# A scan over chunks: spread rows for the decays, gates of the cells turned ahead, cell norm on ScalarE

## What is computed

```
z_a, xbc, dt_raw, z_b, q, k, v, ig, fg, og = split(rmsnorm(x) @ ab_w_in)
# state space mixer: xbc = silu(causal_conv(xbc)); xs, bm, cm = split(xbc); 16 heads of 64, 2 groups
y_a = y_diag(decays, cm, bm, xs * dt) + (cm @ state) * exp(acs) + xs * d_skip
state = state * exp(acs_end) + bm^T @ (decay_to_end * xs * dt)
y_a = rms(y_a * silu(z_a)) * ssd_norm_g                   # rms over each group of 512
# matrix memory mixer: q, k = silu(causal_conv(..)); 4 heads, keys of 128, values of 256
num = (q k^T * w_intra) @ v + w_inter * (q @ c_mem);  den = the same with ones for v
h = num / max(|den|, exp(-m_t)) * sigmoid(og)
c_mem = dec * c_mem + (g * k)^T @ v
y_b = rms(h) * ml_norm_g * silu(z_b)                      # rms over each head of 256
x = x + concat(y_a, y_b) @ ab_w_out
```

## Time and profile before

| | |
|---|---|
| median of 3 runs | 1576.92 us (1575.18 to 1577.39) |
| the profiled execution | 1573.38 us, span 1571.6 us |
| PE busy | 1525.6 us, 97% |
| DVE, ACT, POOL busy | 907.6, 649.0, 566.1 us |
| granted clock, mean | 0.992 |
| projection | 17 to 559 us |
| scan | 561 to 737 us |
| output product in the scan's stage | 737 to 761 us |

### The profile page before, as it was taken

One profiled execution on the slowest core, in us unless ns is written; L12 is line 12 of the kernel. 1 busy time (PEld: TensorE's weight loads), 2 busy tenths in 40 slices (PEclk: granted clock), 3 DMA queues, 4 the chain that ended last, 5 costly groups with the idle time before them and its releaser, 6 DMA issues.

```text
span 1571.6 us, 23657 instructions
## 1 busy us (share of the span) xinstructions
PE 1525.6 (97%) x9114; PEld 1314.0 (84%) x9114; DVE 907.6 (58%) x1484; ACT 649.0 (41%) x1272; POOL 566.1 (36%) x325
## 2 busy tenths in 40 slices
PE   8999999999999999999999999999999999999897
PEld 7798989898999987877788877888888888787686
DVE  7675878684843469999344272345544245554623
ACT  6542534353532233444345252345555333556321
POOL 3245454545344346567565330132212013211110
PEclk9999999999999999999999999999999999999899
DMA  5133333333334345765675330122111112113612
GB/s 178 41 122 94 122 94 121 94 121 94 121 108 135 100 160 186 227 199 175 220 267 201 121 94 14 28 61 76 53 54 34 34 28 80 54 35 114 254 67 107
DMA packets 151085, 176.43 MB, mean 112 GB/s; under 512 B 9671, under 2 KB 126659, under 8 KB 149955
## 3 DMA queue, kind: packets, MB, share of 16 engines
q1 hardware_dynamic: 150810, 174.92, 34.2%
q10 hardware_dynamic: 168, 0.06, 0.0%
HBM read 122.46 MB, written 52.43 MB: 111 GB/s over the span
## 4 chain that ended last, share of the span: by engine, by line
PE 47%; DVE 1%; ACT 1%; issue 1%; DMA 1%; POOL 0%; SPq 0%; POOLq 0%; ACTq 0%; DVEq 0%
PE b_ps L2404 22%; PE b_ps L2449 4%; PE b_ps L2424 4%; PE b_ps L2354 3%; PE b_ps L2356 3%; PE b_ps L2355 3%; PE b_ps L2436 2%; PE b_ps L2506 2%; PE b_ps L2507 2%; PE b_ps L2508 2%; PE b_ps L2457 1%; PE b_ps L2372 0%; DMA b_yy<-z 0%; DMA z<-b_y_T 0%; ACT a_aT L2056 0%
## 5 line engine op out<-in xcount | busy, mean ns | idle before, releaser
L1925 POOL TENSOR_TENSOR b_w<-b_w_raw,b_w 128x1024 fp32r<-128x1024 f32 x66 | 158.4, 2400 | 357.5 <-DVE b_w L2184 253.6
L2404 PE MATMUL b_ps<-a_h_hi,b_w 128*128 128x512 f32 x768 | 265.7, 406 | 2.9 <-DVE a_h_lo L2162 2.9
L393 POOL TENSOR_TENSOR b_w<-b_y_T,b_w 128x1024 fp32r<-128x1024 f32 x54 | 141.1, 2615 | 189.7 <-ACT b_w L451 189.7
L2404 PEld LDWEIGHTS b_ps<-a_h_hi,b_w 128*128 128x128 f32 x768 | 145.0, 189 | 37.1 <-issue 3.9
L2404 PE MATMUL b_ps<-a_h_lo,b_w 128*128 128x512 f32 x384 | 150.6, 392 | 0.0
L941 PE MATMUL b_ps<-b_w,p_hi 128*128 128x256 f32 x768 | 139.2, 283 | 0.0
L700 DVE SCALAR_TENSOR_TENSOR b_w_raw<-p_out_raw,p_cols,b_w_raw 128x1024 f32<-128x1024 f32 x60 | 119.8, 2003 | 12.8 <-ACT b_w_raw L482 11.4
L941 PEld LDWEIGHTS b_ps<-b_w,p_hi 128*128 128x128 f32 x768 | 120.1, 192 | 0.6
L941 PE MATMUL b_ps<-b_w,p_lo 128*128 128x256 f32 x384 | 108.7, 283 | 0.0
L2195 DVE CUSTOM_DVE_ANT_0 b_y_T<-b_ps,a_neg_dist 128x128 f32<-128x128 f32 (+5 forms) x96 | 72.1, 777 | 63.3 <-PE b_ps L2424 52.7
L451 ACT CAST b_w<-b_y_T 128x1024 fp32r<-128x1024 f32 x60 | 62.7, 1045 | 106.5 <-DVE b_y_T L661 55.0
(11 more groups left out here) (417 smaller groups left out, 3616.6 us busy)
## 6 DMA issues: line engine op xcount, KB each, us to landing
b_y_T<-in_ab_w_in SPq DMA_DIRECT2D x33, 512.0 KB, 4.3
tok<-p_out_raw SPq DMA_DIRECT2D x64, 256.0 KB, 2.3
b_w_raw<-in_ab_w_out SPq DMA_DIRECT2D x32, 512.0 KB, 3.7
b_w_raw<-in_c_w_in SPq DMA_DIRECT2D x32, 512.0 KB, 4.1
feat<-b_w_raw SPq DMA_DIRECT2D x20, 512.0 KB, 2.7
c_fe<-feat SPq DMA_DIRECT2D x7, 1280.0 KB, 6.6
yt<-b_y_T SPq DMA_DIRECT2D x8, 1024.0 KB, 10.9
b_y_raw<-yt SPq DMA_DIRECT2D x32, 256.0 KB, 3.9
```

The source lines that it names most:

```text
L393: gp.tensor_tensor(w_lo[s % SLOTS][:, :, :], operand(n, split_of(n, p))[:, :, :], w_hi[s % SLOTS][:, :, :].bitcast(F32), ALU.subtract).the ...
L1925: gp.tensor_tensor(w_lo[:, w, :], w_raw[u % W_RAW][:, :], w_hi[:, w, :].bitcast(F32), ALU.subtract).then_inc(S["l_wlo"], 1)
L2404: mm = pe.matmul(o, x, y, start=(k == 0 and q == 0), stop=(k == KT - 1 and q == 2))
```

## The change

- The vectors (norm gains, taps, biases, d_skip) are laid out by the host as one array of columns, `in_columns`, loaded once into `cols`. The row loads and transposes at the start of the projection and of the scan go, with `gcols` and `d_bc`.
- The two blocks of z_b are computed turned (as the "f" blocks are) and stored turned, in `zt0`. After silu, ScalarE multiplies them by the cells' norm gain (`gains_of_quarter`), a quarter later. In the scan they are loaded turned (`load_gate_cells`) and multiplied in when VectorE turns y (`turn`, part 0), in the place of the gain.
- Spread rows: the running sums are kept as `dec_bd`, 512 wide, with each row only in the 128 columns of its own head of four; one product of 512 columns (`decay_rows`) makes four heads' rows. The same for the cells' rows with `ml_bd` (`d_mlbd`).
- The cells' norm is four copies with a scale on ScalarE (`memory_norm`), in front of decay groups 0 and 1; L1628 on VectorE goes. GpSimd's power for the cells goes in front of `yd`.
- `e_end` goes from VectorE to GpSimd. On VectorE `qs`, `st`, `gk` and y's means go in front of `wt`; the next chunk's tables go in front of the new memory. ScalarE's squares for y stay between decay groups 1 and 2.
- Chunk 0 leaves out the products and sums with the zero memory and state; its scores go first, and its cells' weights behind decay group 0. Chunk 7 leaves out the new memory, state and what they need. Two of the low parts of the output weights go to VectorE.

```diff
+            def gains_of_quarter(n, i, k):
+                if not gate_turned(n):
+                    return
+                c0 = tok_blocks[number[n]][3]
+                for b in (0, 1):
+                    gained[0] += 1
+                    act.wait_ge(S["silu_z"], gained[0])
+                    gain = CELL_GAIN + c0 + 2 * k + b
+                    nc.scalar.activation(area(i, k, b), area(i, k, b), ACT.Copy, scale=cols[:, gain:gain + 1]
+                                         ).then_inc(S["a_out"], 1)
+
...
+                    if kinds[n] == "t" and k == 2:
+                        gains_of_quarter(n, 0, 0)
+                    if after(n, "t") and k < 3:
+                        gains_of_quarter(n - 1, *((1, 1), (1, 0), (0, 1))[k])
...
+                dve.wait_ge(S["heads_ok"], 4)
+                for j in (0, 1):
+                    chain(dve.tensor_tensor(dec_bd[:, j, :, :], mid(g_ps["rows"][:, (2 + j) * P:(3 + j) * P], 4),
+                                            last(keep["of_four"][:, :], P), ALU.mult))
...
-                    if kinds[n] == "f":
+                    if kinds[n] == "f" or gate_turned(n):
...
 def decay_rows(pe, ps, keep, par, q, S):
     bank = 4 + q % 2
-    for k in range(4):
-        h = 4 * q + k
-        pe.matmul(ps[:, bank, k * P:(k + 1) * P], keep["head_sel"][:, h:h + 1].broadcast_to([P, P]),
-                  keep["dec_rows"][:, par * P:(par + 1) * P], start=(k == 0), stop=False, skip_group_check=True)
+    pe.matmul(ps[:, bank, :], keep["head_sel"][:, q:q + 1].broadcast_to([P, P]), keep["dec_bd"][:, par, :],
+              start=True, stop=False, skip_group_check=True)
     pe.matmul(ps[:, bank, :], keep["ident_bf"][:, :], mid(keep["later"][:, :], 4), start=False, stop=True,
...
+def load_gate_cells(sp, chunk, n, into, landed):
+    sp.dma_start(into.rearrange("p (f t) -> p f t", t=P), chunk["zt"][:, :, bass.ds(n * P, P)].rearrange("f p t -> p f t")
+                 ).then_inc(landed, 16)
...
+                sp.wait_ge(S["d_yT"], n * 4 + 2)
+                load_gate_cells(sp, chunk, n + 2, cell_gate[par], in_landed[par])
...
+                rows_of = lambda b: keep["cell_sel"][:, b:b + 1].broadcast_to([P, P])
+                if behind_first(n):
+                    pe.wait_ge(S["d_cmem"], n * 4)
+                    pe.matmul(ps[:, 7, :], rows_of(1), ml_bd, start=True, stop=True).then_inc(S["p_wint"], 1)
+                pe.matmul(ps[:, 6, :], rows_of(0), ml_bd, start=True, stop=False, skip_group_check=True)
...
+                for h in (2, 3, 0, 1):
+                    if h == 3 and behind_first(n) and not is_last(n):
+                        pe.wait_ge(S["d_cdec"], n + 0)
+                    if h < 2:
+                        pe.wait_ge(S["a_dec"], n * 4 + 3 + h)
+                    mm = pe.matmul(ps[:, 4 + h, 0:VW], st[:, h, :], va[par][:, h, :], start=True, stop=not behind_first(n))
+                    if behind_first(n):
+                        mm = pe.matmul(ps[:, 4 + h, 0:VW], qs[:, h, :], cmem[:, h, :], start=False, stop=True)
                     mm.then_inc(S["p_num"], 1)
...
+            def memory_norm(n):
+                act.wait_ge(S["l_rstdm"], n + 1)
+                for h in range(ML_HEADS):
+                    yb = y[:, D + h * ML_V:D + (h + 1) * ML_V]
+                    a = nc.scalar.activation(yb, yb, ACT.Copy, scale=rms[:, 2 + h:3 + h])
+                a.then_inc(S["a_yb"], 1)
...
             def body(n, par, prior):
                 memory_squares(n)
+                memory_norm(n)
                 decays(n + 1, (0, 1))
                 ssd_squares(n)
                 decays(n + 1, (2,))
...
+                if behind_first(n) and not is_last(n):
+                    if not isinstance(n, int) or n > 1:
+                        gp.wait_ge(S["l_sdec"], n - 1)
+                    gp.tensor_tensor(e_end[:, :], dec[:, :, P - 1:P].rearrange("p h a -> p (h a)"),
+                                     g[:, T_EACS:T_EACS + SSD_HEADS], ALU.mult).then_inc(S["l_eend"], 1)
+                    gp.wait_ge(S["l_eend"], n + 0)
+                    gp.wait_ge(S["p_yoff"], n * 2)
+                    gp.wait_ge(S["d_state"], n * 2)
...
+                gp.wait_ge(S["d_meanm"], n + 1)
+                gp.tensor_tensor(rms[:, 2:6], rms[:, 2:6], half[:, 0:4], ALU.pow).then_inc(S["l_rstdm"], 1)
...
-                dve.wait_ge(S["l_sdec"], n + 0)
-                dve.wait_ge(S["a_dec"], n * 4 + 4)
-                dve.tensor_tensor(e_end[:, :], dec[:, :, P - 1:P].rearrange("p h a -> p (h a)"),
-                                  g[:, T_EACS:T_EACS + SSD_HEADS], ALU.mult).then_inc(S["d_eend"], 1)
-
-                dve.tensor_scalar(gk[:, :], wm[:, :, P - 1:P].rearrange("p h a -> p (h a)"), ML_QK ** -0.5, None,
-                                  ALU.mult).then_inc(S["d_gk"], 1)
+                if not is_last(n):
+                    dve.tensor_scalar(gk[:, :], wm[:, :, P - 1:P].rearrange("p h a -> p (h a)"), ML_QK ** -0.5, None,
+                                      ALU.mult).then_inc(S["d_gk"], 1)
+                means()
+                ssd_weights(0)
                 turned()
                 ssd_weights(1)
+                if is_last(n):
+                    low_y(0)
+                    low_y(1)
+                    return
                 dve.wait_ge(S["d_gk"], n + 1)
                 dve.wait_ge(S["p_kT"], n + 1)
                 dve.tensor_tensor(kg[:, :, :], b4(2), last(gk[:, :], P), ALU.mult).then_inc(S["d_kg"], 1)
 
             def turn(n, part, par, prior=0):
...
+                    by = last(gcols[:, 4 * b:4 * b + 4], P) if part else gate_cells(n, par)[:, 4 * b - 8:4 * b - 4, :]
+                    dve.tensor_tensor(y_T[par][:, 4 * b:4 * b + 4, :], b4(i), by, ALU.mult).then_inc(S["d_yT"], 1)
...
+            def low_unit(u):
+                dve.wait_ge(S["w_high"], u + 1)
+                dve.wait_ge(S["l_wlo"], u)
+                dve.tensor_tensor(w_lo[:, slot(u), :], ahead["w_raw"][u % W_RAW][:, :], w_hi[:, slot(u), :].bitcast(F32),
+                                  ALU.subtract).then_inc(S["l_wlo"], 1)
...
+            dve.wait_ge(S["ml_rows"], 4 * 16)
+            dve.tensor_tensor(ml_bd.rearrange("p (h t) -> p h t", t=P), mid(keep["ml_rows"][:, :], 4), last(keep["of_four"][:, :], P),
+                              ALU.mult).then_inc(S["d_mlbd"], 1)
```

More of the change, by code:

```diff
@@ L145, with projection_ab @@
 T_USED, T_ALL = 56, 64
-def projection_ab(nc, keep, ahead, x, w_in, rows, feat_cols, feat_out, tok_blocks, tok_out, vectors, load_first, chunk):
-    nrows = sum(r.shape[0] for r in rows)
+def projection_ab(nc, keep, ahead, x, w_in, columns, feat_cols, feat_out, tok_blocks, turned_out, vectors, load_first, chunk):
     nf, nt = len(feat_cols), len(tok_blocks)
@@ L499, in keep_gates @@
                 nc.scalar.copy(g_st[s], g_bank[s][0:GATES, :]).then_inc(S["g_staged"], 1)
-            at = 0
-            for r in rows:
-                act.dma_start(row_in[at:at + r.shape[0], :], r).then_inc(S["rows_in"], 16)
-                at += r.shape[0]
+            act.dma_start(cols[:, :], columns).then_inc(S["cols_in"], 16)
             for t in range(4):
@@ L1114, in scan_chunks @@
         ident_bf, later = keep["ident_bf"], keep["later"]
-        gcols = m.sb("gcols", [P, AB_OUT_T])
-        d_bc = m.sb("d_bc", [P, SSD_HEADS])
+        gcols, d_bc = keep["cols"][:, SSD_GAIN:SKIP], keep["cols"][:, SKIP:COLUMNS]
         x_tok = m.sb("x_tok", [P, D])
@@ L1434, in _ @@
             ssd_squares(TILES - 1)
+            high_y(3)
             ssd_norm(TILES - 1)
-            for u in range(3, UNITS_RING):
+            high_unit(3)
+            for u in range(4, UNITS_RING):
                 high_y(u)
@@ L1494, in _ @@
             body(TILES - 1, 1, (TILES - 1) // 2, low_unit)
-            for u in range(3, UNITS_RING):
+            gp.wait_ge(S["l_wlo"], 4)
+            for u in range(4, UNITS_RING):
                 low_unit(u)
@@ L1630, in outputs @@
-                a.then_inc(S["d_yb"], 1)
+                if not is_last(n):
+                    next_tables()
+                    dve.wait_ge(S["p_cmem"], n + 1)
+                    for h in range(ML_HEADS):
+                        if behind_first(n):
+                            dve.scalar_tensor_tensor(out=cmem[:, h, :], in0=cmem[:, h, :], scalar=c_dec[:, h:h + 1],
+                                                     in1=ps[:, 4 + h, 0:VW], op0=ALU.mult, op1=ALU.add).then_inc(S["d_cmem"], 1)
+                        else:
+                            dve.tensor_copy(cmem[:, h, :], ps[:, 4 + h, 0:VW]).then_inc(S["d_cmem"], 1)
+                    dve.wait_ge(S["p_state"], n + 1)
+                    if behind_first(n):
+                        dve.wait_ge(S["l_sdec"], n + 0)
+                    for k in (0, 1):
+                        c = slice(k * 512, (k + 1) * 512)
+                        if behind_first(n):
```

(3 more changed lines are left out.)

319 lines of the change are left out of this document (151 added, 168 removed).

## The result

The changed kernel takes 1563.12 us (median of 6 runs, 1561.31 to 1569.09), the kernel before 1576.47 (6 runs, 1575.18 to 1577.39). The ratio is 0.992, 95% interval 0.9903 to 0.9937. The forecast was 1564.6, between 1555 and 1573. The profiled execution took 1563.39 us, its span 1561.7, against 1573.4 and 1571.6 before: 10 us less there, 13.4 in the medians. Of the difference of 3.4 us, 3.1 are in the kernel before alone: its profiled execution, at 1573.4, was quicker than each of its six timed runs.

The account below looks back on a forecast made before the run. It took TensorE to bound the projection and a chain through all four engines to bound the scan. Terms 0.6 + 4.5 + 0.5 + 1.5 + 2.1 + 0.9 + 2.2 = 12.3 us, from 1576.9 to 1564.6 us, range 1555 to 1573.

Parts of the forecast that it names:

- Start: Start of the projection: one load replaces row loads, transpose and copy; gain 0.6 us, bounds 0 and 1.8.
- Projection: z_b's two blocks computed turned, as 512-column instead of 256-column products; gain 4.5 us, bounds 3 and 4.5.
- Row selections: One 512-column product for four saves 0.25 us a group, hidden in the scan; 0.5 us counted at the projection's end.
- Into the scan: Entry to the scan's stage, with copies and fills gone and scores first; gain 1.5 us, bounds 0 and 2.5.
- Chunk 0: First scan chunk, without old memory: 20.99 us becomes 18.9; gain 2.1 us, bounds 1 and 3.5.
- Chunks 1 to 6: Scan chunks 1 to 6: period 21.9 us, with a wait in the second denominator step; gain 0.9 us over six.
- Last chunk: Last scan chunk to the first output product: 15.06 us becomes 12.9; gain 2.2 us, bounds 0 and 5.2.
- A: Scan chunks: the engines' work sets the pace, 27 us saved in all, 1550 us; chance 0.05.
- B: Scan chunks: no wait in the denominators, 21.2 us a chunk, 1560.5 us in all; chance 0.2.
- C: VectorE's third denominator step waits behind GpSimd's state decay: 24.0 us a chunk, 1576.5 to 1578 in all; chance 0.13.
- D: Tail: gains don't reach the end because output-weight loads or the stage's end take them up; 1570 us; chance 0.12.
- One product set takes 68.27 - 62.83 = 5.44 us in this form: Projection: a z_b set costs 5.44 us turned against 5.76 in the other form, 0.32 saved on each of 14 sets.

Follow-up runs that it names:

- the two placed kernels: The changed kernel with p_hi begun 128 bytes past a multiple of 1024 (1564.34 us), and that kernel with z_b's products in token form again (1571.94 us).
- placed: The changed kernel with kept tiles laid out so p_hi begins 128 bytes past a multiple of 1024, gains loaded in two loads: 1564.34 us, ratio 0.9918.
- filled: The changed kernel with fourteen unused identity turns on TensorE in its wait before the scores of chunks 1 to 6: 1570.93 us, ratio 0.9968.
- one more tile: The changed kernel with only a tile of 32 bytes per partition added behind the kept tiles: 1568.6 us.
- second profile: The changed kernel run once more with nothing changed, beside other experiments: 1564.68 us, ratio 0.9933 to the kernel before.

## Why the forecast was right, and where it was not

The forecast time, 1564.6, is 1.5 us from the median. That it is so close is in part luck. The terms sum to 12.3 us, and the profiled pair differs by 10.0, of which 8.3 are where the terms were looked for. The medians differ by 13.4, mostly because the kernel before was profiled in a quick execution. Term by term:

- **Start.** 0.9 us at the first product for 0.6: right.
- **Projection.** Wrong in size, and for a reason that was not in the text. Turned z_b is worth 4.55 us where the tiles are placed as before (the two placed kernels), the term said 4.5. The change itself slowed the 512-column sets that read p tiles, 5.62 us for 5.44, because the new kept tiles moved the p tiles. Placing them gave back 2.5 us. From the first product to the scan's stage the kernel after gained 1.9 us (544.1 to 542.2) and the placed one 4.4, with the row selections at the projection's end in it; the term's stated bounds were 3 to 4.5, and 0.5 for the selections.
- **Row selections.** Hidden inside the scan, as said: four products a group leave the chunk at 21.84. The saving itself was put too high, 0.17 us a group for 0.25, which cost the sum little, as it counted only two groups.
- **Into the scan.** 2.0 for 1.5, within its bounds.
- **Chunk 0.** 20.50 in the profile for 18.9, with falls at 564 and 581.5. Where no fall lies in it it takes 17.5 (placed), 17.9 (filled) and 18.0 (one more tile). The working, which had no falls, was 0.9 to 1.4 us too long; one profile's falls hid that. Which step of it was too long was not looked for.
- **Chunks 1 to 6.** The undisturbed period is 21.84, for 21.9. The squares' place is what holds it there (19.9 with the squares late). The wait in the denominators exists and is worth 0.4 us a chunk. The falls took back 1.5 us over two chunks, which the sum did not have; without falls the six take 130.8 us (placed), a gain of 1.3 for the forecast 0.9.
- **Last chunk.** 12.26 for 12.9, and TensorE's `ydiag` waited 1.84 us for the turns, behind the low parts, as said, though not the 3 us of the forecast. The second profile has 14.19 with a fall in it.

Of the rivals, A is refuted: the engines' work does not set 21.84, and with the chain broken TensorE's work gives 19.9, near A's 19.4 (its own numbers, 20.7 less 1.5, make 19.2). B's case did not occur: the step took 0.76 to 0.92 us in most chunks. C decided nothing in the chunks, where the third step went first by 0.2 us. It does appear in the last chunk once the low parts are moved. D did not occur at the end: between the first output product and the end 1.6 us more were gained, in one pair of profiles, with 11 us at 1.2 GHz there against 21. How the 13.4 us between the medians divide among the parts is not settled by single profiles, since the falls lie elsewhere in each.

So the mechanism of the chunk was right. The step that failed is "One product set takes 68.27 - 62.83 = 5.44 us in this form", taken over unchanged to a kernel whose tiles had moved, where the sets that read p tiles take 5.6.

## What to carry to other kernels

When a chain through several engines sets the period, find the one operation in it that the next stage doesn't need, here the squares in front of the third group, and move that first; work saved on an engine that waits for the chain only becomes idle time. When a wait of a short VectorE operation beside GpSimd is taken away by reordering, list all short VectorE operations with SBUF operands around it: here the wait went to the next one. When a change adds tiles in front of others, compare the pace of untouched products before and after, and try the old offset before looking for another cause.
